# Sample part of a forgetting attention: products in column tiles of 32 and float32, against split fp32r products over the full array

## The chip, the cores and the metric

The kernel runs on one core of a Trainium2 chip. The metric is the device time of one execution in microseconds; three executions of the kernel before gave a median of 3855.15 us (3853.97 to 3856.22). The engines are TensorE (PE in the rows; PEld is its weight load), VectorE (DVE), ScalarE (ACT), GpSimd (POOL) and SyncE (SP), which issues most DMAs.

## The reference, cut to what matters

One step of a two-layer decoder for a prompt of 2048 tokens and for 8 sample sequences of 4 new tokens. The change touches the forgetting attention of layer 0 for the samples: each sequence has 16 pages of 128 cached keys and values (8 heads of 128), found through a page table, and 4 new ones.

```python
s_past = jnp.einsum('bqhd,bkhd->bhqk', q, k_past).astype(jnp.float32) * scale
s_past = s_past + suf[:, :, None, :] + c_new[:, :, :, None]
s_new = jnp.einsum('bqhd,bkhd->bhqk', q, k_new).astype(jnp.float32) * scale
s_new = s_new + (c_new[:, :, :, None] - c_new[:, :, None, :])
...
p = jax.nn.softmax(jnp.concatenate([s_past, s_new], axis=-1), axis=-1).astype(v_new.dtype)
out = (jnp.einsum('bhqk,bkhd->bqhd', p[..., :n_past], v_past)
       + jnp.einsum('bhqk,bkhd->bqhd', p[..., n_past:], v_new))
```

`suf` is a suffix sum of forget gates over the cached keys, `c_new` a running sum over the new ones. Since a softmax does not change when a row gets a constant, `c_new` of the query cancels.

## The kernel before, in words

Layer 0 projects the states with `fox_w_in` in two passes, each over half of the tokens (`project_pass`). The second pass, called p01, has 41 tiles of 128 output columns; each tile takes 48 products of 128x512 (L434), in fp32r with both operands split into a high and a low part: high x high, low x high, high x low. Other work is threaded through the pass as `Work` objects: each is a set of five generators, one for each engine, advanced together by a plan. For `sample_fox` the plan is `[(2, 0), (4, 3), (33, 153)]`: 3 steps between tiles 2 and 4, and 150 between tiles 4 and 33. On each engine the instructions stand in this written order; nothing is reordered, and an engine that waits in `sample_fox` holds up the projection behind it.

One step `s` of `sample_fox` handles one page (128 pages in all, `NPG`), in this order on TensorE: every second step the scores of the last two pages (L1958, L1959, `group`), then 8 transposes of a page of keys (L1973), then the V products of a page of the sequence before (L1987, L1988, `products`). The probabilities of a sequence are transposed once (L1996, L2001), and the output rows are folded (L1943).

The queries of all 8 heads stand in one block matrix `qx`, 4 rows for each head and for the high and low part, so one product gives 64 useful rows of 128. Scores for a pair of pages are 16 products of 256 columns in one PSUM bank. The low rows are then copied by ScalarE (L2032) and added by VectorE (L2110, L2113). Keys are evicted twice from PSUM: a high part by ScalarE (L2025), the rest by VectorE (L2095). Values are split from SBUF in the same way (L2019, L2090). Key pages are loaded by SP four deep (`KR`), value pages by GpSimd three deep (`VR`).

At the start SP loads a mask and two biases with 24 small DMAs (`mask`, `c_key`, `c_qry`, three for each head), and VectorE waits for all of them before its first key copy.

Of the kernel before, what the change touches and what calls it, by code (L numbers as in the profile page):

```python
# [14 lines left out]
P = 128  # L15
# [1665 lines left out]
def sample_gates(nc, stack, room, const, banks, zT, f_row, bias_f, past, lf_sample, sufT, cnew, cnew_q, plan):  # L1681
# [15 lines left out]
    lf, cn = c.sb("lf", [NS, FH]), c.sb("cn", [FH, 2, NS])  # L1697
# [7 lines left out]
    def sp(sp):  # L1705
        for i in range(STEPS):
            if i == 0:
                sp.dma_start(f[:, :], zT[f_row:f_row + FH, SEQ:TOK]).then_inc(f_in, 16)
                sp.dma_start(b_col[:, :], bias_f.unsqueeze(1)).then_inc(f_in, 16)
            if i == 6:  # L1710
                sp.wait_ge(lc_d, 1)
                sp.dma_start(lf_sample.rearrange("b t h -> (b t) h"), lf[:, :]).then_inc(out_d, 16)
                sp.wait_ge(cn_d, TN + 1)
                sp.dma_start(cnew[:, :], cn[:, 0, :]).then_inc(out_d, 16)
                sp.dma_start(cnew_q.rearrange("h (t b) -> h t b", t=TN),
                             cn[:, 1, :].rearrange("h (t b) -> h t b", t=TN)).then_inc(out_d, 16)
            if i == STEPS - 1:
                sp.wait_ge(row_d, 4)
                for q in range(TN):
                    sp.dma_start(sufT.rearrange("(r q) n -> q r n", q=TN)[q], suf_row[:, :]).then_inc(out_d, 16)  # L1720
                sp.wait_ge(out_d, 16 * (3 + TN))
            yield
# [25 lines left out]
    def dve(dve):  # L1748
        for i in range(STEPS):
            if i == 1:  # L1750
# [7 lines left out]
                sums = cn[:, 0, :].rearrange("h (b t) -> h b t", t=TN)  # L1758
# [4 lines left out]
                dve.wait_ge(cn_d, TN)  # L1763
                nc.vector.tensor_copy(cn[:, 1, :].rearrange("h (t b) -> h b t", t=TN), sums).then_inc(cn_d, 1)
# [35 lines left out]
    return Work(STEPS, plan, dict(sp=sp, pool=pool, pe=pe, act=act, dve=dve)), [(out_d, 16 * (3 + TN))]  # L1800


def sample_fox(nc, stack, room, const, banks, zT, gate_row, bT, cache_k, cache_v, page_table, sufT, cnew, cnew_q, v_new, plan, freed):


# [9 lines left out]
    R, LO, NG, NV = FH * TN, 32, PAGES // 2, PAGES + 1  # L1815
    KR, VR = 4, 3
# [18 lines left out]
    room_d, zero_d, mf_d, set_in, kn_in = (c.sem(n) for n in ("room_free", "zeroed", "mask_made", "queries_loaded", "setup_loaded"))  # L1835
    tab_in, tabv_in, set_d, kn_d, bias_d, eye_d, qx_d = (c.sem(n) for n in (
        "table_loaded", "table_v_loaded", "queries_split", "k_new_split", "new_bias_ready", "eye2_made", "queries_placed"))
    k_in, v_in = ([c.sem(f"{n}{u}") for u in range(m)] for n, m in (("k_loaded", KR), ("v_loaded", VR)))
    suf_in = [c.sem(f"suffix_loaded{u}") for u in range(2)]
    kt_d, kth_d, ktl_d, s_done = (c.sem(n) for n in ("k_transposed", "kT_hi_done", "kT_lo_done", "scores_done"))  # L1840
    low_d, hi_d, sc_d = (c.sem(n) for n in ("low_rows_copied", "high_rows_biased", "scores_ready"))
    nm_d, p_d, rr_d, pn_d = (c.sem(n) for n in ("maximum_ready", "exp_done", "inverse_ready", "p_normalised"))
    pt_d, pth_d, ptl_d, vh_d, vl_d = (c.sem(n) for n in ("p_transposed", "pT_hi_done", "pT_lo_done", "v_hi_done", "v_lo_done"))
    pv_d, o_d, x_d, m_d, out_d = (c.sem(n) for n in ("pv_done", "o_copied", "o_transposed", "mixed", "stored"))
# [3 lines left out]
    STEPS = LEAD + PAGES * DB + 22  # L1848

# [5 lines left out]
    def group(s):  # L1855

        g = s // 2 - 1
        return divmod(g, NG) if s % 2 == 0 and 0 <= g < DB * NG else None
# [9 lines left out]
    def sp(sp):  # L1868
        row = lambda r0: zT[r0:r0 + D, cols].rearrange("(h p) n -> p h n", p=P)
        for i in range(STEPS):  # L1870
# [10 lines left out]
            if i == 1:  # L1881
                sp.wait_ge(mf_d, 2)
                for h in range(FH):
                    at = slice(TN * h, TN * h + TN)
                    sp.dma_start(mask[at, :], maskf[:, :]).then_inc(kn_in, 16)
                    sp.dma_start(c_key[at, :, :].rearrange("q b t -> q (b t)"), cnew[h, :].partition_broadcast(TN)).then_inc(kn_in, 16)
                    sp.dma_start(c_qry[at, :], cnew_q[h, :].rearrange("(t b) -> t b", t=TN)).then_inc(kn_in, 16)
# [5 lines left out]
            b = 0 if i == 0 else batch(s, -8)  # L1893
            if b is not None and (b or i == 0):
# [9 lines left out]
    def pool(pool):  # L1904
        def load(y):
            b, p = divmod(y, NV)
            if y >= VR:
                pool.wait_ge(vl_d, y - VR + 1)
# [5 lines left out]
        for i in range(STEPS):  # L1914
            s = i - LEAD
            if i == 0:
# [6 lines left out]
                nc.gpsimd.memset(qx[:, :].bitcast(F32), 0.0).then_inc(zero_d, 1)  # L1923
                nc.gpsimd.memset(pT[:, :].bitcast(F32), 0.0).then_inc(zero_d, 1)
                nc.gpsimd.memset(sc[:, :, W:], 0.0).then_inc(zero_d, 1)
                pool.wait_ge(tabv_in, 16)
            if s == 12:
# [7 lines left out]
    def pe(pe):  # L1935
        for i in range(STEPS):
            s = i - LEAD
            b = batch(s, 36)
            if b is not None:
                pe.wait_ge(o_d, 2 * b + 2)  # L1940
                pe.wait_ge(ptl_d, min(2 * (b + 2), 2 * DB))
                for h in range(FH):
                    last = nc.tensor.matmul(M_BANK[:, h * LO:(h + 1) * LO], o_sb[:, h * P:(h + 1) * P], eye2[:, :], start=True, stop=True)  # L1943
                last.then_inc(x_d, 1)
            if group(s) is not None:
                b, g = group(s)
                if b == 0 and g == 0:
                    pe.wait_ge(zero_d, 3)
                    pe.wait_ge(eye_d, 1)
                    pe.wait_ge(kn_d, 2)  # L1950
                pe.wait_ge(qx_d, 2 * b + 2)
                pe.wait_ge(ktl_d, 2 * s)
                if s > 2:
                    pe.wait_ge(hi_d, NG * b + g + b)
                    pe.wait_ge(low_d, NG * b + g + b)
                for h in range(FH):
# [3 lines left out]
                if g == NG - 1:  # L1960
                    out = S_BANK[:, 2 * P:2 * P + TN]
                    for h in range(FH):
                        q = qx[:, h * P:(h + 1) * P]
                        nc.tensor.matmul(out, q, kn_hi[:, h, TN * b:TN * (b + 1)], start=(h == 0), stop=False)
                        last = nc.tensor.matmul(out, q, kn_lo[:, h, TN * b:TN * (b + 1)], start=False, stop=(h == FH - 1))
                last.then_inc(s_done, 1)
            if 0 <= s < NPG:
                pe.wait_ge(k_in[s % KR], 16 * (s // KR + 1))
                if s:
                    pe.wait_ge(ktl_d, 2 * s)  # L1970
                for n in range(2):
                    for h in range(4):
                        last = nc.tensor.transpose(T_BANKS[n][:, h * P:(h + 1) * P], k_raw[:, s % KR, (4 * n + h) * P:(4 * n + h + 1) * P], ident[:, :])  # L1973
                    last.then_inc(kt_d, 1)
            for b, p in products(s):
                y = NV * b + p
                if p == 0:
                    pe.wait_ge(ptl_d, 2 * b + 1)
                    if b:
                        pe.wait_ge(o_d, 2 * b)  # L1980
                if p == PAGES:
                    pe.wait_ge(ptl_d, 2 * b + 2)
                pe.wait_ge(vl_d, y + 1)
                pr = pT[:, p * 2 * LO:p * 2 * LO + P]
                for n in range(2):
# [589 lines left out]
```

## Time and profile before

| | |
|---|---|
| median of three runs | 3855.15 us |
| profiled execution, span | 3849.1 us |
| TensorE busy | 3479.4 us (90%) |
| VectorE / ScalarE / GpSimd busy | 1792.1 / 1366.2 / 438.3 us |
| pass p01 | about 684 to 1700 us |
| pages of `sample_fox` in it | 741 to 1515 us |

The profiled execution is one more execution, with the hardware profiler on; its span runs from the first to the last instruction. Busy shares are averages over stages with different limits, so what a change in one stage is worth is read from that stage. Matmul records are longer than the distance at which they start, because they are pipelined: the cost of one is the difference between two starts.

### The profile page before, as it was taken

The numbers are of one execution on the slowest core, as the hardware profiler recorded it, in microseconds if no ns is written. First come the engines' busy times: TensorE is split into PE (matmuls) and PEld (weight loads), VectorE is DVE, ScalarE is ACT, GpSimd is POOL, SyncE is SP. The second block draws the span as 40 slices with busy tenths as digits, with TensorE's granted clock in tenths as the row PEclk, the third lists the DMA queues.
The fourth block names the chain that finished last, engine by engine and source line by source line (L and its number), as shares of the span: only waits on it lengthen the run. The fifth ranks groups of instructions, "written<-read, shape, count | busy, mean of one in ns | idle before, by whom it ended". The sixth has DMA issues, their size and how long they took to land. (4 is left out here: it accounts for less than half of the span.)

```text
span 3849.1 us, 53371 instructions
## 1 busy us (share of the span) xinstructions
PE 3479.4 (90%) x19825; PEld 3040.2 (79%) x19825; DVE 1792.1 (47%) x3288; ACT 1366.2 (35%) x2569; POOL 438.3 (11%) x644
## 2 busy tenths in 40 slices
PE   5999899799999999977888889899499889997999
PEld 5999799688888887766777778788499877775887
DVE  3332213256666664536677777422322245474422
ACT  3112322145555553435555555311212254311311
POOL 1320000001111110103332322000000000132000
PEclk9999999899999999988999999999799999997999
DMA  3344333557777765323222220532233243564631
GB/s 123 117 132 151 106 95 101 149 192 242 235 234 242 242 201 159 104 87 118 74 78 75 77 79 27 186 113 80 86 116 111 91 135 123 159 213 147 198 109 57
DMA packets 409310, 515.84 MB, mean 134 GB/s; under 512 B 50743, under 2 KB 298040, under 8 KB 407503
## 3 DMA queue, kind: packets, MB, share of 16 engines
q1 hardware_dynamic: 386215, 444.74, 37.1%
q0 software_dynamic: 22848, 67.78, 5.6%
q8 instruction: 158, 2.59, 0.3%
q14 instruction: 89, 0.73, 0.1%
HBM read 388.57 MB, written 124.22 MB: 133 GB/s over the span
## 5 line engine op out<-in xcount | busy, mean ns | idle before, releaser
L459 ACT ACTIVATE z_st_p<-bank 128x352 f32<-128x352 f32 (+3 forms) x325 | 168.0, 518 | 743.0 <-PE bank L434 742.5
L1600 PE MATMUL bank<-w_hi_o,b_hi_o 128*128 128x512 f32 x816 | 319.4, 391 | 26.7 <-DVE w_lo_o L1659 26.7
L434 PE MATMUL bank<-h00hi,w_hi_p 128*128 128x352 f32 x984 | 323.3, 329 | 17.7 <-DVE w_lo_p L401 7.9
L1601 PE MATMUL bank<-w_hi_o,b_lo_o 128*128 128x512 f32 x816 | 318.7, 391 | 0.0
L1602 PE MATMUL bank<-w_lo_o,b_hi_o 128*128 128x512 f32 x816 | 318.6, 390 | 0.0
L434 PE MATMUL bank<-h00hi,w_lo_p 128*128 128x352 f32 x984 | 317.9, 323 | 0.0
L434 PE MATMUL bank<-h00lo,w_hi_p 128*128 128x352 f32 x984 | 317.8, 323 | 0.0
L399 DVE CAST w_hi_p<-w_raw_p 128x1024 fp32r<-128x1024 f32 (+1 forms) x130 | 89.4, 687 | 448.2 <-PE bank L434 388.5
L434 PE MATMUL bank<-h01hi,w_hi_p 128*128 128x512 f32 x656 | 271.4, 414 | 12.9 <-DVE w_lo_p L401 11.9
L852 DVE TENSOR_TENSOR pT_lo_fa<-bank,pT_hi_fa 128x512 fp32r<-128x512 f32 (+2 forms) x320 | 193.9, 607 | 140.1 <-ACT pT_hi_fa L794 139.2
L434 PE MATMUL bank<-h01lo,w_hi_p 128*128 128x512 f32 x656 | 258.5, 394 | 0.0
L434 PE MATMUL bank<-h01hi,w_lo_p 128*128 128x512 f32 x656 | 258.4, 394 | 0.0
L2095 DVE TENSOR_TENSOR kT_lo_sf<-bank,kT_hi_sf 128x512 fp32r<-128x512 f32 x256 | 164.6, 684 | 179.3 <-ACT kT_hi_sf L2025 179.3
L767 PE MATMUL bank<-ident_const,sc_fa 128*128 128x128 f32 x1088 | 177.3, 279 | 77.0 <-DVE pT_lo_fa L852 58.6
L2025 ACT CAST kT_hi_sf<-bank 128x512 fp32r<-128x512 f32 x256 | 137.7, 590 | 289.7 <-PE bank L1973 289.6
L801 ACT ACTIVATE sc_fa<-sc_fa,nm_fa 128x128 f32<-128x128 f32 (+15 forms) x128 | 154.3, 1206 | 164.4 <-DVE nm_fa L857 164.4
L767 PEld LDWEIGHTS bank<-ident_const,sc_fa 128*128 128x128 f32 x1088 | 123.8, 141 | 108.1 <-DVE pT_lo_fa L852 50.0
L794 ACT CAST pT_hi_fa<-bank 128x512 fp32r<-128x512 f32 (+2 forms) x320 | 156.1, 514 | 140.3 <-PE bank L767 140.1
L434 PEld LDWEIGHTS bank<-h00hi,w_hi_p 128*128 128x128 f32 x984 | 186.4, 189 | 23.0 <-ACT tok_p L453 10.9
L1600 PEld LDWEIGHTS bank<-w_hi_o,b_hi_o 128*128 128x128 f32 x816 | 154.0, 189 | 60.5 <-DVE w_lo_o L1659 27.4
L2090 DVE TENSOR_TENSOR v_lo_sf<-v_raw_sf,v_hi_sf 128x1024 fp32r<-128x1024 f32 x128 | 156.0, 1219 | 97.9 <-ACT v_hi_sf L2019 97.5
L434 PE MATMUL bank<-h10hi,w_hi_p 128*128 128x352 f32 x576 | 187.6, 326 | 8.5 <-DVE w_lo_p L401 8.5
(349 smaller groups left out, 8753.5 us busy)
## 6 DMA issues: line engine op xcount, KB each, us to landing
k_raw_sf<-in_cache_fox_k SPq DMA_DIRECT2D x128, 512.0 KB, 4.3
v_raw_sf<-in_cache_fox_v POOLq DMA_DIRECT2D x128, 512.0 KB, 4.7
z<-z_st_p SPq DMA_DIRECT2D x112, 512.0 KB, 3.1
w_raw_p<-in_fox_w_in SPq DMA_DIRECT2D x80, 512.0 KB, 5.3
b_raw_o<-bT SPq DMA_DIRECT2D x32, 768.0 KB, 6.1
w_raw_p<-in_pool_w_in SPq DMA_DIRECT2D x48, 512.0 KB, 5.2
out<-tok_p SPq DMA_DIRECT2D x64, 256.0 KB, 2.5
w_raw_o<-in_w_out SPq DMA_DIRECT2D x24, 512.0 KB, 4.7
```

What stands on the lines that cost most here:

```text
L434: last = nc.tensor.matmul(bank[:, 0:width], wt[:, u, k, :], h[:, k, at0:at0 + width], start=(m == 0), stop=(m == MM - 1))
L459: nc.scalar.activation(z_st[0:rows_t, t % 2, at0:at0 + width], bank[0:rows_t, 0:width], tiles[t][2]).then_inc(z_read, 1)
L767: last = nc.tensor.transpose(T_BANKS[g % 2][:, n * P:(n + 1) * P], sc[:, qt % NB, (4 * p + n) * P:(4 * p + n + 1) * P], ident[:, :])
L794: nc.scalar.copy(pT_hi[:, J % 2, 4 * p:4 * p + nk, a * P:(a + 1) * P], T_BANKS[g % 2][:, 0:nk * P].rearrange("p (n q) -> p n q", q=P)).the ...
L801: nc.scalar.activation(sc[:, qs % NB, 0:w], sc[:, qs % NB, 0:w], ACT.Exp, bias=nm[:, qs % NB:qs % NB + 1], accum_out=rs[:, J % 2, qs % QB: ...
L852: nc.vector.tensor_tensor(pT_lo[at], T_BANKS[g % 2][:, 0:nk * P].rearrange("p (n q) -> p n q", q=P), pT_hi[at].bitcast(F32), ALU.subtract) ...
L1600: nc.tensor.matmul(bank(t, half)[:, :], bh, w_hi[:, k, cols], start=(k == 0), stop=False)
L1601: nc.tensor.matmul(bank(t, half)[:, :], bl, w_hi[:, k, cols], start=False, stop=False)
L1602: last = nc.tensor.matmul(bank(t, half)[:, :], bh, w_lo[:, k, cols], start=False, stop=(k == NK - 1))
L2025: nc.scalar.copy(kT_hi[:, 4 * n:4 * n + 4, s % 2 * P:(s % 2 + 1) * P], T_BANKS[n][:, :].rearrange("p (h n) -> p h n", h=4)).then_inc(kth_d, 1)
L2090: nc.vector.tensor_tensor(v_lo[:, y % 2, :], v_raw[:, y % VR, :], v_hi[:, y % 2, :].bitcast(F32), ALU.subtract).then_inc(vl_d, 1)
L2095: nc.vector.tensor_tensor(kT_lo[at], T_BANKS[n][:, :].rearrange("p (h n) -> p h n", h=4), kT_hi[at].bitcast(F32), ALU.subtract).then_inc(k ...
```

## The change

Heads 2j and 2j+1 of a sequence go to column tile j of the array, that is to output rows 32j to 32j+7; the query of a head is its own matrix of 32 columns, with 4 of them filled. Each product is plain float32 with 32 output columns, and four consecutive products go to the four column tiles. Scores of a pair of pages are 8 products of 256 columns; a page of V is 4 products, one for each pair of heads, of 256 columns (the two heads of the pair against both, of which half is used). The splits of keys, values, queries and probabilities are gone: keys are copied once from PSUM, half by ScalarE and half by VectorE, and values are read as they were loaded. The scores are biased and their maximum is found in one VectorE instruction for a pair. The probabilities stand in 128 rows; 17 full transposes turn them in five groups. They are not normalised before the V product; the output is scaled instead. The scores of the new keys are computed once at the start for all sequences. The query's own bias is left out. Value pages are four deep, and the suffix sums come in four loads for each sequence.

```diff
+    JT, CT, NP2, NV = 4, 32, PAGES // 2, PAGES + 1
+    KR, VR = 4, 4
     W = PAGES * P
+    NG = (NV + 3) // 4
...
-    qs_hi, qs_lo, kn_hi, kn_lo = (c.sb(n, [P, FH, NS], F32R) for n in ("qs_hi", "qs_lo", "kn_hi", "kn_lo"))
-    qx = c.sb("qx", [P, FH * (P + TN) + P], F32R)
+    qx = c.sb("qx", [P, DB, FH, CT])
     k_raw, v_raw = c.sb("k_raw", [P, KR, D]), c.sb("v_raw", [P, VR, D])
-    kT_hi, kT_lo = (c.sb(n, [P, FH, 2 * P], F32R) for n in ("kT_hi", "kT_lo"))
-    v_hi, v_lo = (c.sb(n, [P, 2, D], F32R) for n in ("v_hi", "v_lo"))
-    low, low_n = c.sb("low", [LO, 2 * P]), c.sb("low_n", [LO, TN])
-    sc = c.sb("sc", [LO, 2, NV * P])
-    pT = c.sb("pT", [P, (NV + 1) * 2 * LO], F32R)
-    o_sb = c.sb("o_sb", [2 * LO, D])
-    eye2 = c.sb("eye2", [2 * LO, LO])
-    nm, rs, rr = (c.sb(n, [LO, 2]) for n in ("nm", "rs", "rr"))
-    c_key, c_bias, mask = c.sb("c_key", [R, DB, TN]), c.sb("c_bias", [R, DB, TN]), c.sb("mask", [R, TN])
-    c_qry, maskf = c.sb("c_qry", [R, DB]), c.sb("maskf", [TN, TN])
+    kT = c.sb("kT", [P, 2, FH, 2 * P])
+    sc = c.sb("sc", [P, 2, NV * P])
+    pT = c.sb("pT", [P, NV, P])
...
+            if i == 1:
+                sp.wait_ge(mf_d, 2)
+                sp.wait_ge(zero_d, 4)
+                for h in range(FH):
+                    sp.dma_start(mask[rows(h), :], maskf[:, :]).then_inc(new_in, 16)
+                    sp.dma_start(c_key[rows(h), :, :].rearrange("q b t -> q (b t)"), cnew[h, :].partition_broadcast(TN)).then_inc(new_in, 16)
+            b = 0 if i == 1 else batch(s, -5)
+            if b is not None and (b or i == 1):
                 if b >= 2:
-                    sp.wait_ge(pt_d, 2 * (b - 1))
-                sp.dma_start(sc[0:R, b % 2, 0:W], sufT[b * R:(b + 1) * R, :]).then_inc(suf_in[b % 2], 16)
+                    sp.wait_ge(pt_d, NG * (b - 1))
+                for j in range(JT):
+                    r0 = (b * FH + 2 * j) * TN
+                    sp.dma_start(sc[CT * j:CT * j + 2 * TN, b % 2, 0:W], sufT[r0:r0 + 2 * TN, :]).then_inc(suf_in[b % 2], 16)
...
-                pool.wait_ge(vl_d, y - VR + 1)
+                pool.wait_ge(pv_d, y - VR + 1)
...
+                pe.wait_ge(qx_d, 2)
+                pe.wait_ge(kn_in, 16)
+                for b in range(DB):
+                    for g in range(2):
+                        for j in range(JT):
+                            h = 2 * j + g
+                            last = nc.tensor.matmul(M_BANK[CT * j:CT * (j + 1), TN * b:TN * (b + 1)], qx[:, b, h, :],
+                                                    kn_raw[:, h, TN * b:TN * (b + 1)], start=(g == 0), stop=(g == 1))
+                last.then_inc(new_d, 1)
...
-                for h in range(FH):
-                    q = qx[:, h * P:(h + 1) * P]
-                    nc.tensor.matmul(S_BANK[:, 0:2 * P], q, kT_hi[:, h, :], start=(h == 0), stop=False)
-                    last = nc.tensor.matmul(S_BANK[:, 0:2 * P], q, kT_lo[:, h, :], start=False, stop=(h == FH - 1))
...
+                if q == 0:
+                    pe.wait_ge(p_d, b + 1)
+                if b or q:
+                    pe.wait_ge(pth_d, NG * b + q)
+                else:
+                    pe.wait_ge(newc_d, 1)
+                if q == 2 and b:
+                    pe.wait_ge(m_d, b)
+                for n in range(min(4, NV - 4 * q)):
+                    last = nc.tensor.transpose(M_BANK[:, n * P:(n + 1) * P], sc[:, b % 2, (4 * q + n) * P:(4 * q + n + 1) * P], ident[:, :])
+                last.then_inc(pt_d, 1)
...
+            if pair(s) is not None:
+                b, n = pair(s)
+                G = NP2 * b + n
+                pe.wait_ge(ka_d, 2 * G + 2)
+                pe.wait_ge(kv_d, 2 * G + 2)
+                if G:
+                    pe.wait_ge(sc_d, G)
+                for g in range(2):
+                    for j in range(JT):
+                        h = 2 * j + g
+                        last = nc.tensor.matmul(S_BANK[CT * j:CT * (j + 1), 0:2 * P], qx[:, b, h, :], kT[:, G % 2, h, :], start=(g == 0), stop=(g == 1))
+                last.then_inc(s_done, 1)
...
-                pr = pT[:, p * 2 * LO:p * 2 * LO + P]
-                for n in range(2):
-                    vs = slice(n * 512, (n + 1) * 512)
-                    nc.tensor.matmul(O_BANKS[n][:, :], pr, v_hi[:, y % 2, vs], start=(p == 0), stop=False)
-                    last = nc.tensor.matmul(O_BANKS[n][:, :], pr, v_lo[:, y % 2, vs], start=False, stop=(p == PAGES))
...
+                if p == 0 and b >= 2:
+                    pe.wait_ge(o_d, b - 1)
+                if p % 4 == 0:
+                    pe.wait_ge(pth_d, NG * b + p // 4 + 1)
+                pe.wait_ge(v_in[y % VR], 16 * (y // VR + 1))
+                for j in range(JT):
+                    last = nc.tensor.matmul(O_BANKS[b % 2][CT * j:CT * (j + 1), 0:2 * P], pT[:, p, CT * j:CT * (j + 1)],
+                                            v_raw[:, y % VR, 2 * P * j:2 * P * (j + 1)], start=(p == 0), stop=(p == PAGES))
...
+                nc.scalar.copy(pT[:, 4 * q:4 * q + n, :], M_BANK[:, 0:n * P].rearrange("p (n r) -> p n r", r=P)).then_inc(pth_d, 1)
...
+                nc.vector.tensor_tensor_reduce(out=dst, in0=S_BANK[:, 0:2 * P], in1=dst, scale=1.0, scalar=LOWEST, op0=ALU.add, op1=ALU.max,
+                                               accum_out=mx[:, b % 2, n:n + 1]).then_inc(sc_d, 1)
...
+                nc.vector.tensor_scalar(o_sb[:, :], O_BANKS[b % 2][:, 0:2 * P], rr[:, b % 2:b % 2 + 1], None, ALU.mult).then_inc(o_d, 1)
```

The two orders below are TensorE's at the same place, a step with scores in the middle of the stage; names ending in `_sf` are `sample_fox`'s, the `bank` tiles are PSUM, and L434 is the projection. First before, the end of the scores, a page of key transposes, the V products, and the small transposes of the probabilities:

```order
L1958 MATMUL bank<-kT_hi_sf,qx_sf 128x256
L1959 MATMUL bank<-kT_lo_sf,qx_sf 128x256
L1973 MATMUL bank<-ident_const,k_raw_sf 128x128 x8
L1987 MATMUL bank<-v_hi_sf,pT_sf 128x512
L1988 MATMUL bank<-v_lo_sf,pT_sf 128x512
L1987 MATMUL bank<-v_hi_sf,pT_sf 128x512
L1988 MATMUL bank<-v_lo_sf,pT_sf 128x512
...
L1996 MATMUL bank<-ident_const,sc_sf 128x32 x16
L434 MATMUL bank<-h01hi,w_hi_p 128x512
```

Then the changed kernel, where the lines are those of the changed file: a group of four full transposes of the probabilities, the key transposes, the scores in eight products and V in four.

```order
L434 MATMUL bank<-h01hi,w_lo_p 128x512
L1971 MATMUL bank<-ident_const,sc_sf 128x128 x4
L1979 MATMUL bank<-ident_const,k_raw_sf 128x128 x8
L1991 MATMUL bank<-kT_sf,qx_sf 32x256 x8
L2001 MATMUL bank<-v_raw_sf,pT_sf 32x256 x4
L434 MATMUL bank<-h01hi,w_hi_p 128x512
```

The scores moved behind the key transposes, next to the V products; 16 products became 8 and 4 became 4, each with 32 output rows of 256 columns instead of 128 of 256 or 512.

On ScalarE the same stage, before, stands as follows, over two steps, with the split of V in each:

```order
L2038 ACTIVATE sc_sf,rs_sf<-sc_sf,nm_sf 32x2052
L2055 CAST v_hi_sf<-v_raw_sf 128x1024
L2019 CAST v_hi_sf<-v_raw_sf 128x1024
L2025 CAST kT_hi_sf<-bank 128x4x128 x2
L2032 COPY low_sf<-bank 32x256
L2045 CAST pT_sf<-bank 128x16x32
L2062 COPY o_sb_sf<-bank 64x512 x2
```

In the changed kernel two steps read:

```order
L2033 ACTIVATE sc_sf,rs_sf<-sc_sf,nm_sf 128x2052
L2020 COPY kT_sf<-bank 128x4x128
L2027 COPY pT_sf<-bank 128x512
L459 ACTIVATE z_st_p<-bank 128x512
L2020 COPY kT_sf<-bank 128x4x128 x2
L2027 COPY pT_sf<-bank 128x512
```

The V splits, the copies of low rows and one of each two key copies are gone from ScalarE; the four-page copies of the transposed probabilities are new.

## Rows read from the trace of the kernel before

**Rows 1.** The page: the head, and busy time of each engine.

```profile
span 3849.1 us, 53371 instructions
...
PE 3479.4 (90%) x19825; PEld 3040.2 (79%) x19825; DVE 1792.1 (47%) x3288; ACT 1366.2 (35%) x2569; POOL 438.3 (11%) x644
```

**Rows 2.** Windows: us, busy time by engine, granted clock, DMA share, GB/s.

```profile
835.00:1400.00 565.00, 555.98 (x3411) 479.79 (x3410) 363.46 (x522) 296.86 (x474) 59.49 (x109) 1.00 0.73 236
1400.00:1515.00 115.00, 111.16 (x569) 91.50 (x568) 58.49 (x68) 53.02 (x76) 12.90 (x24) 0.97 0.54 166
```

**Rows 3.** Waits of PE from 741 to 1515 us: total, times, longest.

```profile
PE bank L1973 <- DVE kT_lo_sf L2095: 14.5, 6, 13.0
PE bank L1958 <- DVE qx_sf L2102: 4.4, 7, 0.8
```

**Rows 4.** Timeline of PE, two pages: start us, us, instruction.

```profile
997.48 1.03 PE L1973 MATMUL bank<-ident_const,k_raw_sf 128*128 128x128 f32 x8
998.27 0.48 PE L1987 MATMUL bank<-v_hi_sf,pT_sf 128*128 128x512 f32 x1
...
999.28 0.39 PE L434 MATMUL bank<-h01hi,w_hi_p 128*128 128x512 f32 x1
...
1001.39 0.39 PE L1958 MATMUL bank<-kT_hi_sf,qx_sf 128*128 128x256 f32 x1 [0.59 <-DVE qx_sf L2102]
1001.62 0.28 PE L1959 MATMUL bank<-kT_lo_sf,qx_sf 128*128 128x256 f32 x1
1001.73 0.28 PE L1958 MATMUL bank<-kT_hi_sf,qx_sf 128*128 128x256 f32 x1
...
1003.39 1.04 PE L1973 MATMUL bank<-ident_const,k_raw_sf 128*128 128x128 f32 x8
1004.18 0.47 PE L1987 MATMUL bank<-v_hi_sf,pT_sf 128*128 128x512 f32 x1
```

**Rows 5.** Timeline of PE: what comes once for each sequence.

```profile
929.37 1.97 PE L1943 MATMUL bank<-eye_sf,o_sb_sf 64*128 64x32 f32 x16
931.26 0.39 PE L1958 MATMUL bank<-kT_hi_sf,qx_sf 128*128 128x256 f32 x1
...
1092.54 1.18 PE L1996 MATMUL bank<-ident_const,sc_sf 32*128 32x32 f32 x16
1093.65 0.50 PE L434 MATMUL bank<-h01hi,w_hi_p 128*128 128x512 f32 x1
...
1098.42 0.24 PE L2001 MATMUL bank<-ident_const,sc_sf 32*128 32x32 f32 x1
1098.59 0.50 PE L434 MATMUL bank<-h01hi,w_hi_p 128*128 128x512 f32 x1
...
1439.84 0.25 PE L1964 MATMUL bank<-kn_hi_sf,qx_sf 128*128 128x4 f32 x1
1439.95 0.25 PE L1965 MATMUL bank<-kn_lo_sf,qx_sf 128*128 128x4 f32 x1
```

**Rows 6.** True float32 products: timeline of PE, and durations ns min/median/max.

```profile
700.63 0.38 PE L1797 MATMUL bank<-ones_const,ex_sg 128*64 128x128 f32 x2
700.85 0.38 PE L1796 MATMUL bank<-after_sg,lfp_sg 128*64 128x128 f32 x2
...
1549.28 1.02 PE L1236 MATMUL bank<-dg_ma,ones_const 128*128 128x512 f32 x2
...
L1236 PE MATMUL bank<-dg_ma,ones_const x64: 590/591/592, 1549.3 to 3343.2; 128*128 128x512 f32 x64
```

**Rows 7.** Timeline of the start: SP's queue, then DVE.

```profile
743.37 0.38 SPq L1887 DMA_DIRECT2D c_qry_sf<-cnew_q  x1
...
753.75 0.29 DVE L2079 CAST kn_hi_sf<-kn_raw_sf 128x256 fp32r<-128x256 f32 x1 [20.66 <-DMA c_qry_sf<-cnew_q]
```

**Rows 8.** Durations of the exponential, ns min/median/max.

```profile
L2038 ACT ACTIVATE sc_sf<-sc_sf,nm_sf x8: 2004/2010/2017, 831.5 to 1444.0; 32x2052 f32<-32x2052 f32 x8
```

**Rows 9.** DMA issues from 835 to 1400 us: count, KB each, us to landing.

```profile
k_raw_sf<-in_cache_fox_k SPq DMA_DIRECT2D x103, 512.0 KB, 4.4
```

More of the change, by code:

```diff
@@ L1757, in dve @@
                 news = f[:, :].rearrange("h (b t) -> h b t", t=TN)
[L1758 removed]
+                sums = cn[:, :].rearrange("h (b t) -> h b t", t=TN)
                 nc.vector.tensor_copy(sums[:, :, 0], news[:, :, 0]).then_inc(cn_d, 1)
@@ L1848, in sample_fox, with rows @@
     STEPS = LEAD + PAGES * DB + 22
+    def rows(h):
+        return slice(CT * (h // 2) + TN * (h % 2), CT * (h // 2) + TN * (h % 2 + 1))
     def batch(s, at):
@@ L1853, in batch, with pair, turn @@
         return b if rest == 0 and 0 <= b < DB else None
-    def group(s):
+    def pair(s):
         g = s // 2 - 1
-        return divmod(g, NG) if s % 2 == 0 and 0 <= g < DB * NG else None
+        return divmod(g, NP2) if s % 2 == 0 and 0 <= g < DB * NP2 else None
+    def turn(s):
+        for b in range(DB):
+            q, rest = divmod(s - PAGES * b - 18, 2)
+            if rest == 0 and 0 <= q < NG:
+                return b, q
+        return None
     def products(s):
@@ L1937, in pe @@
             s = i - LEAD
-            b = batch(s, 36)
+            if i == 2:
+                pe.wait_ge(qx_d, 2)
+                pe.wait_ge(kn_in, 16)
+                for b in range(DB):
+                    for g in range(2):
[4 more added lines that the diff above has]
+                last.then_inc(new_d, 1)
@@ L1939, in pe @@
+            b = batch(s, 37)
             if b is not None:
[L1940 to L1943, printed above, removed]
+                pe.wait_ge(o_d, b + 1)
+                pe.wait_ge(pth_d, min(NG * (b + 1) + 2, NG * DB))
+                for g in range(2):
+                    last = nc.tensor.transpose(M_BANK[:, g * P:(g + 1) * P], o_sb[:, g * P:(g + 1) * P], ident[:, :])
@@ new lines, in pe @@
+            if turn(s) is not None:
+                b, q = turn(s)
+                if q == 0:
[9 more added lines that the diff above has]
+                last.then_inc(pt_d, 1)
@@ new lines, in act, with dve @@
+            yield
+    def dve(dve):
+        for i in range(STEPS):
+            s = i - LEAD
+            if i == 2:
+                dve.wait_ge(new_in, 16 * 2 * FH)
+                nc.vector.tensor_tensor(c_bias[:, :, :], mask[:, :].unsqueeze(1).broadcast_to([P, DB, TN]), c_key[:, :, :], ALU.subtract).then_inc(bias_d, 1)
+                dve.wait_ge(new_d, 1)
+                nc.vector.tensor_copy(snew[:, :, :], M_BANK[:, 0:DB * TN].rearrange("p (b t) -> p b t", t=TN)).then_inc(newc_d, 1)
+                dve.wait_ge(bias_d, 1)
+                dve.wait_ge(newc_d, 1)
+            if 0 <= s < NPG:
+                dve.wait_ge(kt_d, 2 * s + 2)
+                if s % 2 == 0 and s >= 4:
+                    dve.wait_ge(s_done, s // 2 - 1)
+                nc.vector.tensor_copy(kT[:, s // 2 % 2, 4:8, s % 2 * P:(s % 2 + 1) * P], T_BANKS[1][:, :].rearrange("p (h n) -> p h n", h=4)).then_inc(kv_d, 1)
+            if pair(s) is not None:
+                b, n = pair(s)
+                G = NP2 * b + n
+                dve.wait_ge(s_done, G + 1)
+                if n == 0:
+                    dve.wait_ge(suf_in[b % 2], 16 * JT * (b // 2 + 1))
+                dst = sc[:, b % 2, n * 2 * P:(n + 1) * 2 * P]
+                nc.vector.tensor_tensor_reduce(out=dst, in0=S_BANK[:, 0:2 * P], in1=dst, scale=1.0, scalar=LOWEST, op0=ALU.add, op1=ALU.max,
+                                               accum_out=mx[:, b % 2, n:n + 1]).then_inc(sc_d, 1)
+                if n == NP2 - 1:
+                    nc.vector.tensor_tensor_reduce(out=sc[:, b % 2, W:W + TN], in0=snew[:, b, :], in1=c_bias[:, b, :], scale=1.0, scalar=LOWEST,
+                                                   op0=ALU.add, op1=ALU.max, accum_out=mx[:, b % 2, NP2:NP2 + 1]).then_inc(bias_d, 1)
+                    dve.wait_ge(sc_d, G + 1)
+                    dve.wait_ge(bias_d, b + 2)
+                    nc.vector.tensor_reduce(nm[:, b % 2:b % 2 + 1], mx[:, b % 2, :], axis=AX.X, op=ALU.max, negate=True).then_inc(nm_d, 1)
@@ L2147, in dve @@
+                nc.vector.tensor_tensor(to(out_all), own, to(g_all), ALU.mult).then_inc(m_d, 1)
             yield
```

264 lines of the change are left out of this document (60 added, 204 removed).

## The prediction

> **What bounds the kernel now.** I read the page first, then the windows of the pass in which the sample part runs, then the waits of TensorE there, and last its timeline over single pages. The page gives a span of 3849.1 us with TensorE busy 90% of it [rows 1]. The sum below is made against the profiled execution, whose span is 3849.1 us; the median of the runs, 3855.15 us, is 6.05 us above it, and I carry every difference over to the median unchanged. A difference under 0.2% (7.7 us) could not be told from no change.
>
> The change lives only in the second pass over layer 0, so only that stretch matters. Between 835 and 1400 us TensorE is busy 556 of 565 us at full clock, VectorE 363, ScalarE 297, and the DMA engines 73% [rows 2]. 103 pages of keys are issued there [rows 9], which is 5.49 us for a page. So TensorE's own instruction stream sets the pace; work taken from VectorE and ScalarE (the splits of V, the low halves of K) is worth nothing by itself, and each microsecond taken from or given to TensorE counts. Real waits of TensorE are few: 14.5 us for VectorE's key copies, 13.0 of them one stall at the start, and 4.4 us for the placing of the queries [rows 3].
>
> What does TensorE spend on a page? Take differences between starts, because records overlap. Eight key transposes take 0.79 us (997.48 to 998.27). The V products of a page take 1.01 us (998.27 to 999.28). The scores of a pair of pages take 2.00 us (1001.39 to 1003.39), at 0.12 us for each of 16 products of 256 columns, with 0.1 us for the change of work in front [rows 4]. So scores and V cost 2.00 + 2 x 1.01 = 4.02 us for two pages. The rest of the page time is the projection, which the change leaves alone.
>
> **The change part by part.** *The price of a float32 product.* The changed products are plain float32 instead of split fp32r. The trace has such products: each is recorded twice. Two of them with 128 columns start 0.22 us apart (700.63, 700.85), so one record takes 0.11 us; with 512 columns two records span 1.02 us and one lasts 0.591, so they start 0.43 us apart [rows 6]. Half of that is 0.215 us for a record of 256 columns, 0.43 us for a product. The changed kernel has 8 such products for a pair's scores (16 records) and 4 for a page of V (8 records).
>
> *How many lie side by side.* This is the one unknown that decides, and no row of before shows it: its products with 64 output columns all go to one column tile [rows 6]. The bounds are: none side by side, 16 x 0.215 = 3.44 us for a pair and 8 x 0.215 = 1.72 for a page of V; all four at once, 4 x 0.215 = 0.86 and 2 x 0.215 = 0.43. Between them lies a middle case. The two records of one product use the same tile, so the second must follow the first. If records also start in program order, the second half of head 0 holds back head 2's first half; each half overlaps only the first half of the next product. A chain of n products then takes (n + 1) x 0.215 us: two tiles at work, not four. I take the middle: every row of before shows TensorE starting products in the order written.
>
> The Trainium skill, "TensorE: Matmul & The Clock Gate", Part 3, says that matmuls keep program order in start and end, and it also reports 2.38 times the speed for three column tiles with 512 columns. The start order agrees with this trace; the speed-up is shown by no row here. By the quoted speed-up read as nearly full overlap the time would be that of the first rival; by the order rule applied to the double records it is my forecast.
>
> In the middle case a step with scores has scores and V in one chain of 12 products: 13 x 0.215 + 0.1 = 2.90 us. A step with V alone: 5 x 0.215 + 0.1 = 1.18 us. Two pages: 4.07 against 4.02 us, +0.05, over 64 pairs **+3 us**. The eight extra products for the new V rows: 8 x (1.18 - 1.01) = **+1 us**. So the part that looks like the gain is worth nothing: half the array time saved by tiles is spent by float32.
>
> *Work once for each of 8 sequences.* Removed or replaced: 16 records that fold the output halves, 1.89 us (929.37 to 931.26); 17 small transposes of the probabilities, 1.11 + 0.17 us, and 0.11 us twice in the product behind them, which lasts 0.50 us, not 0.39; 16 records against the new keys at 0.11 us, 1.76 us [rows 5, 4]. That is 5.15 us. In their place stand 17 full transposes at 0.10 us [rows 4] in five groups with 0.1 us in front of each, 2.2 us, and two output transposes, 0.3 us. 2.65 us less, times 8: **-21 us**.
>
> *The start.* TensorE stalls 13.0 us there [rows 3], since VectorE's first preparation runs only at 753.75 us, behind 24 small loads on SP's queue; eight of them (c_qry, 0.38 us each to issue) go [rows 7], at most 3 us. Against that the 64 products with the new keys now come first on TensorE: 128 records at 0.11 us at most [rows 5], 14 us, but ahead of the 13 us stall and mostly inside it. Bounds -3 and +2 us; I take **-2 us**. The fourfold loads of suffix sums and larger clears on GpSimd stand in the same stall; without it they would cost about 2 us. Behind SP's waits there are only key and weight loads, four deep.
>
> *Waits.* The wait for placing queries goes, **-4 us** [rows 3]. New ones: the first transposes of the probabilities come one step earlier behind the exponential of 2.0 us [rows 8], eight times. Part of it lies beside the page's remaining products (5.49 less 0.79 and 2.01 leaves 2.7 us of other work for a page), so from 0 to 2 us each; I take 0.5, **+4 us**. V's load is now awaited by TensorE itself, but it is issued four pages ahead, over 20 us, against the 4.4 us a key page of the same size takes to land [rows 9]. VectorE and ScalarE lose the V splits and half of the copies, worth 0 while both have 200 us and more of slack in the window [rows 2]; with that slack gone they would be the bound instead of TensorE.
>
> Sum: 3 + 1 - 21 - 2 - 4 + 4 = -19 us; 3855 - 19 = **3836 us**.
>
> **The rivals.** *All four tiles at once.* Scores and V take 6 x 0.215 + 0.1 = 1.39 us in one step and 0.53 in the other, 1.92 for two pages instead of 4.02: 64 x 2.10 = -134 us, new V rows -4, the rest as above -23: 3694 us. A page then takes some 4.2 us, so the DMA share of 0.73 [rows 2] would rise to about 0.95. What DMA gives back is between 0 (133 MB at the 323 GB/s that 236 at 73% imply need 413 us, TensorE 434) and 46 us (at 277 GB/s, a sixth above today). I take 20: 3714 us. For it: four tiles are written so that neighbours never share one. Against: the double records.
>
> *No overlap* (the other side). If the products of different column tiles run one after another, a step with scores takes 24 records and 0.1 us (5.26), one with V alone 8 and 0.1 (1.82): 7.08 against 4.02 us for two pages, 64 x 3.06 = +196, new V rows +6, the rest -23: 4034 us. The place is TensorE between two projection pieces. It decides from 0.230 us for each half-step of the chain (18 half-steps in two pages, 64 times, 15 ns each use up the 19 us), so little loss of overlap is enough. For it: no row of before shows any two products sharing the array; against: nothing but the tiles' separateness.
>
> *A drain at every change of shape.* With half overlap as forecast, TensorE changes between full array and column tiles four times in two pages, 256 times. A product of 256 columns lasts 0.28 us but the next starts 0.12 us later [rows 4]; if each change must let the pipe run empty, that is 0.16 us, up to 41 us in all, and 3836 + 41 = 3877; I take 3870 us, as part is in the 0.1 us already counted. It decides from 19 / 256 = 0.07 us for a change.
> The Trainium skill, "TensorEngine Tiling (Array Packing)", Key Properties, says that a change of tiling mode drains the engine; that is this rival's mechanism, and no row of before has a column-tiled stream to test it.
>
> **How the numbers follow.** Half overlap 0.38, all four 0.27, no overlap 0.20, drain 0.15. Half overlap by itself runs from 3815 to 3855 us (waits 0 to 2 us each, the start, 5 ns in a half-step). The range leaves out only the case without overlap and takes the bounds of the others: 3694 to 3885 us. Faster: 0.27 + 0.31 of half overlap + 0.01 = 0.59; within 0.2%: 0.06 + 0.03 = 0.09; slower: 0.20 + 0.11 + 0.01 = 0.32.
>
> **What would show it.** In the trace after: starts of score and V records in a chain (about 0.215 us for a head if half overlapped, 0.11 if all four, 0.43 if none); a page time near 5.3 us; about 2.5 us for what comes once in a sequence; TensorE still busy nearly all of the window with VectorE and ScalarE far below before. The prediction is wrong if head products start much nearer or farther than 0.215 us, if TensorE waits for DMA, or if the product after a tiled stream starts late.

## The result and the profile after

The changed kernel takes 3715.9 us (median of 4 runs, 3713.86 to 3717.89) against 3854.56 us for the kernel before in the same comparison: a ratio of 0.9645, interval 0.9631 to 0.9658. That is 139 us less, outside the interval of half overlap and 2 us from the time I had given for the rival of all four tiles. The profiled execution has a span of 3712.2 us, 136.9 us under that of before [rows 1].

The first view is again the windows, here over the pages of the changed kernel (columns as in [rows 2]):

```profile
835.00:1260.00 425.00, 421.11 (x3352) 303.18 (x3351) 121.53 (x259) 112.83 (x193) 53.16 (x100) 1.00 0.89 289
1260.00:1370.00 110.00, 109.00 (x782) 74.47 (x780) 23.48 (x45) 25.15 (x44) 15.38 (x29) 1.00 0.73 232
```

The clock granted to TensorE is 1.00 in both rows. TensorE is busy 421 of 425 us, so it still sets the pace. VectorE fell to 122 and ScalarE to 113 us, and DMA moves 289 GB/s with a share of 0.89. The DMA view of the same window has the number of pages:

```profile
k_raw_sf<-in_cache_fox_k SPq DMA_DIRECT2D x94, 512.0 KB, 5.1
v_raw_sf<-in_cache_fox_v POOLq DMA_DIRECT2D x94, 512.0 KB, 5.7
```

94 pages in 425 us are 4.52 us for a page, against 5.49 us before [rows 2, 9]. The difference of 0.97 us times 128 pages is 124 us: nearly the whole gain lies in the steady page time. Landing takes 5.1 instead of 4.4 us.

Where in a page? The timeline of TensorE over two pages, to be laid beside [rows 4]:

```profile
1002.42 0.39 PE L434 MATMUL bank<-h01hi,w_lo_p 128*128 128x512 f32 x1
1002.66 1.03 PE L1979 MATMUL bank<-ident_const,k_raw_sf 128*128 128x128 f32 x8
1003.62 1.07 PE L1991 MATMUL bank<-kT_sf,qx_sf 128*32 128x256 f32 x16
1004.51 0.61 PE L2001 MATMUL bank<-v_raw_sf,pT_sf 128*32 128x256 f32 x8
1005.05 0.50 PE L434 MATMUL bank<-h01hi,w_hi_p 128*128 128x512 f32 x1
1005.39 0.40 PE L434 MATMUL bank<-h01lo,w_hi_p 128*128 128x512 f32 x1
...
1006.55 1.03 PE L1979 MATMUL bank<-ident_const,k_raw_sf 128*128 128x128 f32 x8
1007.51 0.64 PE L2001 MATMUL bank<-v_raw_sf,pT_sf 128*32 128x256 f32 x8
1008.09 0.50 PE L434 MATMUL bank<-h01hi,w_hi_p 128*128 128x512 f32 x1
1008.42 0.40 PE L434 MATMUL bank<-h01lo,w_hi_p 128*128 128x512 f32 x1
```

And from the kernel before, the projection behind its V products:

```profile
999.28 0.39 PE L434 MATMUL bank<-h01hi,w_hi_p 128*128 128x512 f32 x1
999.51 0.39 PE L434 MATMUL bank<-h01lo,w_hi_p 128*128 128x512 f32 x1
```

Read the starts. Sixteen score records take 0.89 us (1003.62 to 1004.51), eight V records 0.54 and 0.58 us: 2.01 us for two pages where the kernel before took 4.02. With 0.215 us for a record and four tiles at work, 16 records are 4 x 0.215 = 0.86 us; with two at work, by the rule of the forecast, they would have been 9 x 0.215 = 1.94. So four tiles run at once. But the work on both sides of the tiles got dearer. The eight key transposes ahead of a tiled stream take 0.96 us instead of 0.79, and the first projection product behind one starts 0.34 us before the second instead of 0.23. That is 2 x (0.17 + 0.11) = 0.56 us for two pages. The net gain here is 4.02 - 2.01 - 0.56 = 1.45 us for two pages, 93 us over 64 pairs.

The waits of TensorE from 741 to 1370 us, against [rows 3]:

```profile
PE bank L1979 <- DVE kT_sf L2051: 6.1, 1, 6.1
PE bank L1971 <- ACT sc_sf L2033: 2.4, 2, 1.5
PE bank L434 <- ACT tok_p L453: 2.2, 9, 0.2
PE bank L423 <- ACT z_st_p L459: 1.0, 4, 0.3
```

The stall at the start fell from 13.0 to 6.1 us, the wait for the queries is gone, the new wait for the exponential is 2.4 us in all, and no wait for a DMA stands in the list. These four lines are the whole list, 11.7 us together. The list of before has nine lines and 28.5 us.

### The profile page after: what moved, and what is told of

The parts are those of the page before. It is cut to its first block and busy times, and to the rows that moved or that the text cites. A ratio compares the mean times of both kernels' runs of the same rounds, so it can differ in the third digit from the quotient of the medians.

```text
span 3712.2 us, 53435 instructions
## 1 busy us (share of the span) xinstructions
PE 3358.9 (90%) x20257; PEld 2850.6 (77%) x20257; DVE 1505.9 (41%) x2987; ACT 1151.0 (31%) x2242; POOL 442.1 (12%) x645
## 5 line engine op out<-in xcount | busy, mean ns | idle before, releaser
L434 PE MATMUL bank<-h00hi,w_hi_p 128*128 128x352 f32 x984 | 323.9, 329 | 17.2 <-DVE w_lo_p L401 7.7
L434 PE MATMUL bank<-h00hi,w_lo_p 128*128 128x352 f32 x984 | 318.8, 324 | 0.0
L434 PE MATMUL bank<-h00lo,w_hi_p 128*128 128x352 f32 x984 | 318.6, 324 | 0.0
L434 PE MATMUL bank<-h01hi,w_hi_p 128*128 128x512 f32 x656 | 283.4, 432 | 13.8 <-DVE w_lo_p L401 11.4
L434 PE MATMUL bank<-h01hi,w_lo_p 128*128 128x512 f32 x656 | 259.5, 396 | 0.0
L434 PE MATMUL bank<-h01lo,w_hi_p 128*128 128x512 f32 x656 | 259.1, 395 | 0.0
L2051 DVE COPY kT_sf<-bank 128x512 f32<-128x512 f32 x128 | 88.5, 692 | 373.1 <-PE bank L1979 373.1
L434 PEld LDWEIGHTS bank<-h00hi,w_hi_p 128*128 128x128 f32 x984 | 187.1, 190 | 22.0 <-ACT tok_p L453 10.7
L434 PEld LDWEIGHTS bank<-h01hi,w_hi_p 128*128 128x128 f32 x656 | 124.1, 189 | 93.7 <-issue 54.0
L844 DVE CUSTOM_DVE_ANT_0 sc_fa<-bank,decay_fa 128x512 f32<-128x512 f32 (+2 forms) x320 | 193.1, 603 | 3.0 <-PE bank L730 1.9
L434 PE MATMUL bank<-h10hi,w_hi_p 128*128 128x352 f32 x576 | 187.3, 325 | 7.3 <-DVE w_lo_p L401 7.3
```

What stands on the lines that cost most here:

```text
L434: last = nc.tensor.matmul(bank[:, 0:width], wt[:, u, k, :], h[:, k, at0:at0 + width], start=(m == 0), stop=(m == MM - 1))
L844: nc.vector.tensor_tensor_reduce(out=sc[:, b, k0:k0 + w], in0=S_BANKS[g % 4][:, 0:w], in1=decay[:, k0:k0 + w], scale=1.0, scalar=LOWEST, o ...
L2051: nc.vector.tensor_copy(kT[:, s // 2 % 2, 4:8, s % 2 * P:(s % 2 + 1) * P], T_BANKS[1][:, :].rearrange("p (h n) -> p h n", h=4)).then_inc(k ...
```

## The experiments

The question was why my order argument failed, and whether the rest of the account holds. Theory 1 is a repaired form of my own: the two records of a product are one unit, units start in program order. Theory 2: each column tile works through its own products, whatever stands between them for other tiles. All are edits of the changed kernel. Each comparison has its own runs of the kernel before: a median of 3851.98 us for the two orders, the scores over the full array and V for two pages at once; 3849.61 us for the scores in one tile, V over the full array and the half pages; 3851.11 us for the last run.

**The two products of a tile in a row.**

```diff
-                for g in range(2):
-                    for j in range(JT):
+                for j in range(JT):
+                    for g in range(2):
```

> The changed kernel with the two loops over the eight score products swapped: the two products of a column tile now follow each other (tile 0, 0, 1, 1, 2, 2, 3, 3). Nothing else changes. Theory 1 (the two records of a float32 product are one unit; units start in program order and a unit waits until its tile is free): a tile's second product waits 0.43 us and holds back the next tile, so the eight start at 0, 0.43, 0.43, 0.86, 0.86, 1.29, 1.29, 1.72 us; scores plus V of a step take 1.29 us longer, 64 times: about +82 us on 3716, so 3798 us. Theory 2 (each tile has its own queue, and the order between tiles does not matter): no change, 3716 us. My failed theory (single records in strict order) would give 13 half-steps of 0.215 us for the scores, about 3840 us.

Measured: 3714.88 us, ratio 0.964 (0.9624 to 0.9656), as in the changed kernel. The timeline of TensorE:

```profile
1003.13 1.03 PE L1979 MATMUL bank<-ident_const,k_raw_sf 128*128 128x128 f32 x8
1004.10 1.09 PE L1991 MATMUL bank<-kT_sf,qx_sf 128*32 128x256 f32 x16
1004.98 0.64 PE L2001 MATMUL bank<-v_raw_sf,pT_sf 128*32 128x256 f32 x8
```

The scores take 0.88 us, not the 2.15 us of theory 1 or the 2.8 us of the forecast's order. Theory 1 and my first theory are both out: four records of one tile in a row hold nothing back.

**Two tiles in turn, then the other two.**

```diff
-                for g in range(2):
-                    for j in range(JT):
+                for j0 in (0, 2):
+                    for g in range(2):
+                        for j in (j0, j0 + 1):
```

> The changed kernel with the score products in the order of tiles 0, 1, 0, 1, 2, 3, 2, 3. Theory 1 (units in program order, each waits for its tile): pairs start at 0, 0.43 (together with the first pair of tiles 2 and 3) and 0.86 us, so a step with scores is 0.43 us longer, 64 times: +28 us, 3744 us. Theory 2 (a queue for each tile): no change, 3716 us.

Measured: 3713.9 us, ratio 0.9641 (0.9625 to 0.9657), no change against the changed kernel, where theory 1 asked for 28 us more. Theory 2 again.

**Scores over the full array.**

```diff
-                        last = nc.tensor.matmul(S_BANK[CT * j:CT * (j + 1), 0:2 * P], qx[:, b, h, :], kT[:, G % 2, h, :], start=(g == 0), stop=(g == 1))
+                    last = nc.tensor.matmul(S_BANK[:, 0:2 * P], qx[:, b, h - h % 4:h - h % 4 + 4, :].rearrange("p h r -> p (h r)"), kT[:, G % 2, h, :], start=(h == 0), stop=(h == FH - 1))
```

> The scores are computed without column tiles: each of the eight float32 products uses 128 output columns (the query matrices of four heads at once) and accumulates into all 128 rows, so the scores are not those of the reference; everything behind them is the same in shape. If the overlap of column tiles brought the gain: 16 records of 0.215 us, 3.44 us for a pair instead of 0.89, 64 times: +163 us, 3879 us, slower than the kernel before. If the gain came from the lighter evictions and the dropped splits instead, the time stays near 3716 us.

Measured: 3872.78 us, ratio 1.0055 (1.0038 to 1.0072): 157 us over the changed kernel and slower than before. Its timeline:

```profile
1002.89 3.62 PE L1989 MATMUL bank<-kT_sf,qx_sf 128*128 128x256 f32 x16
1006.44 0.64 PE L1999 MATMUL bank<-v_raw_sf,pT_sf 128*32 128x256 f32 x8
```

The scores take 3.55 us from start to start, 16 x 0.216 us and 0.1 us for the change of shape behind them. VectorE and ScalarE have the same instructions here as in the changed kernel, so lighter evictions and dropped splits alone buy nothing: without the tiles, float32 scores cost more than the split ones.

**All scores in one tile.** The edit keeps 32 output columns and sends every product to tile 0, except for the first pair of pages.

```diff
+                for h in range(FH if G else 0):
+                    last = nc.tensor.matmul(S_BANK[0:CT, 0:2 * P], qx[:, b, h, :], kT[:, G % 2, h, :], start=(h == 0), stop=(h == FH - 1))
-                for g in range(2):
+                for g in range(0 if G else 2):
```

> All eight score products of a pair (except for the very first pair) go to column tile 0, with 32 output columns as before; 96 of the 128 rows of scores keep old values, so the output is not that of the reference. If tiles overlap only because they are different tiles, 16 records of 0.216 us follow each other, 3.45 us for a pair instead of 0.89: +163 us, 3879 us, as in the run with the full array (3873). If narrow products were cheap by themselves, near 3716 us. With two queues of different depth in one tile nothing changes in this sum.

Measured: 3874.96 us, ratio 1.0067 (1.005 to 1.0084). Narrow products are not cheap by themselves; only different tiles overlap. The timeline shows more than the sum asked for:

```profile
1005.95 3.42 PE L1989 MATMUL bank<-kT_sf,qx_sf 128*32 128x256 f32 x15
1009.00 0.42 PE L2003 MATMUL bank<-v_raw_sf,pT_sf 128*32 128x256 f32 x3
1009.21 0.38 PE L1989 MATMUL bank<-kT_sf,qx_sf 128*32 128x256 f32 x1
1009.24 0.78 PE L2003 MATMUL bank<-v_raw_sf,pT_sf 128*32 128x256 f32 x5
```

Three V records start at 1009.00 us, and the sixteenth score record, written before them, starts at 1009.21. All 55 steps of this run that hold both scores and V show the same: three V records, the last score record, then the other V records. This is theory 2 seen directly: products went ahead of an earlier one that had to wait for tile 0. Their number, three, fits the three free tiles; the rows do not name the tile of a record.

**V over the full array.**

```diff
-                    last = nc.tensor.matmul(O_BANKS[b % 2][CT * j:CT * (j + 1), 0:2 * P], pT[:, p, CT * j:CT * (j + 1)],
-                                            v_raw[:, y % VR, 2 * P * j:2 * P * (j + 1)], start=(p == 0), stop=(p == PAGES))
+                    last = nc.tensor.matmul(O_BANKS[b % 2][:, 0:2 * P], pT[:, p, :],
+                                            v_raw[:, y % VR, 2 * P * j:2 * P * (j + 1)], start=(p == 0 and j == 0), stop=(p == PAGES and j == JT - 1))
```

> The V products without column tiles: each of the four float32 products of a page has 128 output columns and accumulates into all 128 rows, so the output is not that of the reference. 8 records of 0.216 us are 1.73 us for a page instead of 0.54 in the steps with scores and 0.58 in the others; two of the four changes of shape in two pages go (0.1 to 0.14 us each). 64 x (3.46 - 1.12 - 0.25) = +134 us and 8 x 1.2 = +9 us for the new V rows: about 3859 us, no faster than before. If the V products were bound by the arrival of value pages instead, less than +50 us.

Measured: 3862.49 us, ratio 1.0035 (1.0021 to 1.0049); 3859 was expected. So scores and V each need the tiles: in float32 over the full array, either of them alone makes the kernel slower than before.

**Half of each value page.**

```diff
+                w = D if y < VR else D // 2
-                pool.dma_start(v_raw[:, y % VR, :], cache_v[ds(n, 1), :, :, :].rearrange("o t h d -> (o t) (h d)")).then_inc(v_in[y % VR], 16)
+                pool.dma_start(v_raw[:, y % VR, 0:w], cache_v[ds(n, 1), :, :, :].rearrange("o t h d -> (o t) (h d)")[:, 0:w]).then_inc(v_in[y % VR], 16)
```

> The changed kernel with value pages loaded only in their first 512 columns (the first four loads are whole), so the output is not that of the reference; a fourth of the cache traffic is gone and the DMA share of 0.89 should fall to about 0.75. My term (DMA gives back 20 us once it is near its limit): about 3696 us. Rival (DMA hidden fully, since TensorE never waits for it in the trace): 3716 us, within 5 us.

Measured: 3714.08 us, ratio 0.9647 (0.9631 to 0.9663), no change. The window from 835 us on (columns as above) shows that the load did fall, from a share of 0.89 and 289 GB/s:

```profile
835.00:1240.00 405.00, 401.43 (x3194) 289.09 (x3193) 115.32 (x244) 105.66 (x182) 51.06 (x95) 1.00 0.75 232
```

DMA at a share of 0.89 costs nothing; the 20 us that I had the full-overlap rival give back are not there.

**V for two pages at once.**

```diff
-            for b, p in products(s):
+            for b, p in (products(s - 1) + products(s) if s % 2 == 0 else []):
```

> The V products of two pages are done together in the steps with scores, right behind them, so TensorE changes between full array and column tiles twice for two pages instead of four times; the number of products is the same. If each change costs what the trace after shows (key transposes last 0.96 us instead of 0.79 where tiles follow, the projection's first product starts 0.34 us before its second instead of 0.23): 128 changes fewer, 0.14 to 0.28 us each, 18 to 36 us less: about 3690 us. If these gaps are a cost of the records alone and not of time, 3716 us. Rival against it: value pages arrive in pairs and too late, and TensorE waits for them: slower than 3716 us.

Measured: 3695.44 us, ratio 0.9596 (0.958 to 0.9612), 20 us under the changed kernel and the fastest here. The timeline:

```profile
1004.47 1.04 PE L1979 MATMUL bank<-ident_const,k_raw_sf 128*128 128x128 f32 x8
1005.44 1.07 PE L1991 MATMUL bank<-kT_sf,qx_sf 128*32 128x256 f32 x16
1006.33 1.05 PE L2001 MATMUL bank<-v_raw_sf,pT_sf 128*32 128x256 f32 x16
1007.30 0.50 PE L434 MATMUL bank<-h01hi,w_hi_p 128*128 128x512 f32 x1
...
1008.80 1.04 PE L1979 MATMUL bank<-ident_const,k_raw_sf 128*128 128x128 f32 x8
1009.59 0.48 PE L434 MATMUL bank<-h01hi,w_hi_p 128*128 128x512 f32 x1
1009.90 0.40 PE L434 MATMUL bank<-h01lo,w_hi_p 128*128 128x512 f32 x1
```

Call a stretch of products in column tiles, between products over the full array, a visit. Both pages of V take 0.97 us instead of 0.54 + 0.58, key transposes without tiles behind them are back at 0.79 us instead of 0.96, and the projection behind them starts 0.31 us before its second product instead of 0.34: 0.35 us for the visit that is gone. The trace of the changed kernel has 137 visits in the sample part, this one 73. Against its own runs of the kernel before, the gain is 156.5 us where the changed kernel has 138.7: 18 us, or 20 by the medians of the two kernels. Over 64 visits that is 0.28 to 0.32 us each.

**One visit more.** The opposite edit: the V block of TensorE's program is moved, unchanged, in front of the key transposes.

```diff
+            for b, p in products(s):
...
             if 0 <= s < NPG:
                 pe.wait_ge(k_in[s % KR], 16 * (s // KR + 1))
...
-            for b, p in products(s):
```

> The changed kernel with the V products of a step moved in front of the key transposes. In a step with scores TensorE then enters and leaves the column tiles twice (V, then transposes, then scores) instead of once; in the other steps the count stays. If one visit to the tiles costs 0.29 us (18.5 us for 64 visits fewer, as measured when V was done for two pages at once), 64 more cost 18 us: about 3734 us. If that gain came from something else (a fuller chain of products, fewer waits), 3716 us.

Measured: 3730.68 us, ratio 0.9687 (0.9671 to 0.9703), 15 us over the changed kernel by the medians, 18 us by the gains over each one's own runs of before (120.4 against 138.7). I had counted 64 visits more, but the trace has 191, only 54 more: the scores of the first pages come before any V product and stand alone either way. That makes 0.27 to 0.34 us for a visit. The timeline shows the step with two visits:

```profile
1000.59 0.64 PE L1981 MATMUL bank<-v_raw_sf,pT_sf 128*32 128x256 f32 x8
1001.16 1.09 PE L1990 MATMUL bank<-ident_const,k_raw_sf 128*128 128x128 f32 x8
1002.18 1.07 PE L2002 MATMUL bank<-kT_sf,qx_sf 128*32 128x256 f32 x16
1003.18 0.50 PE L434 MATMUL bank<-h01hi,w_hi_p 128*128 128x512 f32 x1
```

The transposes between two tiled streams take 1.02 us, where 0.96 with one stream behind them and 0.79 with none were read above. Taking visits away and adding them move the time by nearly the same amount for each, so the price is real. In both runs the waits for the exponential are longer, 5.8 and 5.7 us instead of 2.4, which makes the saving look a little smaller and the cost a little larger.

## Why the prediction was wrong

**TensorE as the bound: right.** 421 of 425 us busy after the change, and taking load from DMA changed nothing. The lighter VectorE and ScalarE were worth nothing by themselves, as the run with full-array scores shows.

**The price of a record: right.** 0.215 us was worked out from products of other widths; with the full array 16 records run at 0.216 us each.

**How many lie side by side: the step that failed.** I wrote that the second record of a product must follow the first and that, "if records also start in program order, the second half of head 0 holds back head 2's first half", and took that because every row of before shows TensorE starting products in the order written. That was read from a trace without a row of two products in different column tiles; it says nothing about such products. What the runs show in its place: four tiles at work, 0.89 us for 16 records where two at work would have taken 1.94. The order of the eight products makes no difference (two runs), and V products start ahead of an earlier score product (one trace, 55 steps). The rule in the Trainium skill, "TensorE: Matmul & The Clock Gate", Part 3, that matmuls keep program order in their starts does not hold in that trace (1009.00 us before 1009.21); the measurement decides. So "nothing is reordered", said of the kernel before, is true of the written order, not of the starts in different column tiles. The Trainium skill, "TensorEngine Tiling (Array Packing)", Key Properties, says that tiles operate independently, and the 0.89 us for 16 records agree. Which mechanism inside TensorE does it (a queue for each tile, or a choice among waiting products) these runs do not separate. The term was +3 us for scores and V; measured on the two pages above and taken 64 times, it is -93 us, with the dearer work on both sides of the tiles in it. The term for the new V rows was +1 us. They lie in the same visit as a page, so they cost the 0.43 us that a second page took in the run with two at once (0.97 - 0.54): 8 x (0.43 - 1.01) = -5 us.

**A visit to the tiles: the rival's mechanism, beside another's.** I gave each change of shape 0.1 us in the forecast and up to 0.16 us as a rival of its own, and let it stand only beside half overlap. The runs show full overlap and a price together, some 0.3 us for a visit. The Trainium skill, "TensorEngine Tiling (Array Packing)", Key Properties, says that a change of tiling mode drains the engine. The trace agrees in that a change costs time (0.96 instead of 0.79 us for the key transposes ahead of one); whether the array runs empty it does not show, since the ends of its TensorE records are modelled. This is what the full-overlap rival left out: two pages took 2.01 + 0.56 = 2.57 us where it had 1.92, and 64 x 0.65 = 41 us. So its 3694 us before DMA were too low, and the 20 us that it took for DMA were wrong, as the run with half pages shows. That its 3714 us came out close is luck: errors of opposite sign.

**Once for each sequence: right, a little small.** In the trace after, a group of four transposes of the probabilities takes 0.43 us and no gap stands between it and the key transposes, where 0.1 us for each group was counted. The lines of TensorE:

```profile
1110.14 0.60 PE L1971 MATMUL bank<-ident_const,sc_sf 128*128 128x128 f32 x4
1110.58 1.04 PE L1979 MATMUL bank<-ident_const,k_raw_sf 128*128 128x128 f32 x8
...
1117.19 0.38 PE L1958 MATMUL bank<-ident_const,o_sb_sf 128*128 128x128 f32 x2
1117.40 1.04 PE L1979 MATMUL bank<-ident_const,k_raw_sf 128*128 128x128 f32 x8
...
1139.25 0.27 PE L1971 MATMUL bank<-ident_const,sc_sf 128*128 128x128 f32 x1
1139.36 1.04 PE L1979 MATMUL bank<-ident_const,k_raw_sf 128*128 128x128 f32 x8
```

Four groups and a single one are 4 x 0.44 + 0.11 = 1.87 us, and 0.21 us for the output: 2.1 us against 5.15, so 24 us less, not 21.

**The start: mis-sized.** I took 2 us; the stall fell by 6.9 us. Of that I had counted at most 3 us, for the eight loads that go. The lines of TensorE after, then VectorE's first key copies, after and before:

```profile
739.38 1.25 PE L1950 MATMUL bank<-kn_raw_sf,qx_sf 128*32 128x4 f32 x128
740.56 0.50 PE L434 MATMUL bank<-h01hi,w_hi_p 128*128 128x512 f32 x1
743.43 1.03 PE L1979 MATMUL bank<-ident_const,k_raw_sf 128*128 128x128 f32 x8
...
747.05 0.60 PE L1979 MATMUL bank<-ident_const,k_raw_sf 128*128 128x128 f32 x4
753.72 1.11 PE L1979 MATMUL bank<-ident_const,k_raw_sf 128*128 128x128 f32 x4 [6.07 <-DVE kT_sf L2051]
...
752.98 0.68 DVE L2051 COPY kT_sf<-bank 128x512 f32<-128x512 f32 x1
...
756.71 1.28 DVE L2095 TENSOR_TENSOR kT_lo_sf<-bank,kT_hi_sf 128x512 fp32r<-128x512 f32 x2
```

VectorE begins its copies 3.7 us earlier and needs one, not two, before TensorE may go on. TensorE restarts at 753.72 instead of 758.14 us, 4.4 us earlier, and stops some 2.5 us later. The 128 records of the new keys, which I had bounded by 14 us, take 1.18 us (739.38 to 740.56), 9 ns each. Four tiles side by side would explain 14 / 4 = 3.5 us; what makes them cheaper still, no run here separates.

**Waits.** -4 us for the queries stands; the exponential cost 2.4 us, not 4. Small waits that the forecast left out went too, the largest of them this one, which is 1.0 us after:

```profile
PE bank L423 <- ACT z_st_p L459: 3.7, 9, 1.2
```

With the measured terms: -93 - 5 - 24 - 7 - 4 + 2 = -131 us, of 136.9 between the two spans. The two lists of waits hold most of the rest: they sum to 28.5 us before and 11.7 after, 16.8 less, where -7 - 4 + 2 = -9 stands in the sum. That is 8 us more, against 1 us for the records of the new keys: -138 us. A microsecond either way is within what such readings can give.

## What to carry to other kernels

In float32, put narrow products in different column tiles and four of them run in the time of one, in each of the three orders tried here; without tiles the same float32 products cost more than the split ones they replace. Gather what goes to the tiles into few visits, since each one cost some 0.3 us here: a one-line regrouping was worth another 18 to 20 us. And when an argument rests on "the trace always shows it so", ask whether the trace contains the case in which it could be otherwise.

## What was not expected of the hardware

Products of different column tiles pass each other: three V records started 0.21 us before a score record that was written ahead of them. Starts in the four tiles lie so close that sixteen records span 1.07 us with 0.38 us for one. And the DMA engines ran at a share of 0.89 and 289 GB/s, with pages landing in 5.1 instead of 4.4 us, while no wait of TensorE for a load stands in the list of waits.
